# Hybrid decoder layer: attention outputs one unit later at step changes, row pieces in one run on GpSimd, and first output-stage tiles loaded from within attention

## The chip, the cores and the metric

The kernel runs on one core of one Trainium2 chip. The metric is the device time of one execution in microseconds. Engines are called PE (matmul), PEld (PE's weight loads), DVE (VectorE), ACT (ScalarE), POOL (GpSimd) and SP (the engine that issues nearly all DMAs).

## The reference, cut to what matters

One layer: an adaLN-modulated RMSNorm, one input projection, three mixers side by side (forgetting attention with 8 heads of 64, RWKV-7 with 4 heads, pooling), a SiLU gate, an output projection, a second RMSNorm and a gated residual. Sequence 4096, width 1024, batch 1. The change touches the attention and the seam to the output projection:

```python
s = jnp.einsum('bhqd,bhkd->bhqk', qh[:, :, q0:L], kh[:, :, :L])
s = s + cum[:, :, q0:L, None] - cum[:, :, None, :L]
p = jax.nn.softmax(jnp.where(causal, s, -jnp.inf), axis=-1)
outs.append(jnp.einsum('bhqk,bhkd->bhqd', p, vh[:, :, :L]))
...
y = jnp.concatenate([y_fox, y_rwkv, y_pool], axis=-1) * jax.nn.silu(g)
x = x + gate * rms_norm(y @ w_out[l], norm_post[l])
```

## The kernel before, in words

Five stages run one after the other, with a barrier of all engines between them: prepare, project, recur (RWKV and pooling), attend, output. They hand data on through scratch tensors in HBM: m.QK and m.V (queries, keys, values), m.G (gates), m.Y (mixer outputs before the gate).

**attend** (L1734 to L2268). A loop of TURNS = 4 turns does two heads each, u = 0 and 1. A head has NB = 8 blocks of 512 queries; block b of head u is a *step* s, 16 in a turn. A step goes over its 4(b+1) key tiles of 128; one key tile of a step is a *unit* k, NQK = 288 in a turn, 1152 in all. The list `start` holds the first unit of each step. On the last four units of a step, the causal diagonal, the width falls from 512 to 384, 256 and 128.

What one unit costs each engine:

- PE computes the scores psc (L2110 and L2112, and the mask product L2108 on the diagonal) into one of two PSUM banks; then the *ahead* work; then `output(k - PV_LAG)`: the product of probabilities and values of the unit five before (PV_LAG = 5), 8 matmuls at full width (L2091, L2093) into the two banks po, which hold all four query tiles of a step.
- ACT turns psc into p (the exponential, L2021, in one of NP = 8 buffers). At step changes it also copies po to oev (`evacuate`, two copies, L2013), after its exponential of unit start+4; PE may begin the po of the next step only then (the wait on o_ev in `output`, where x == 0).
- POOL computes plo, the low part of p that the second product needs (L1999), for three units of four; DVE does it for the fourth, k % 4 == 2 (L2224).
- DVE normalizes finished steps (`result`, `result_scaled`, L2230 to L2237).

The *ahead* work is how the softmax gets its maximum: PE computes a query-major score tile into one of NM = 4 banks pm (L2043, one for each unit, for a step AHEAD = 48 units on), DVE takes its maximum (L2164). When a step's maxima are all there its *row* is made: POOL adds an offset (`sums`, L1958, one unit after), DVE takes the largest (`largest`, L2244, two units after), POOL splits the result in three float16 pieces with seven small dependent operations (`pieces`, L1972 to L1984: four of them three units after, three of them four units after), PE transposes them into pm (`turn_row`, L2052, ROW_LAG = 7 units after) and DVE copies the row into qb (`copy_row`, L2191, COPY_LAG = 8). Each engine takes its instructions in the written order, so POOL's pieces stand ahead of the plo of their unit, and behind the wait for DVE's largest. Rows do not complete evenly: within a turn they are complete at units 11, 35, 63, 95, 99, 107, 119, 135 and at 144 more than each.

Before the loop stands a prologue with 48 such score tiles and the 4 rows that they complete. In it DVE does the row's steps itself: `m_step`, seven chained instructions (L2171 to L2183), then it waits for PE's transposes and copies.

At the start of attend SP loads qa, ka, the factors, qb, kb and v of head 0. At its end SP waits until the last attention outputs have landed in m.Y, then for its other loads, and the barrier follows.

**output** (L2271 to L2454). For each tile of 128 rows: load y, g and x, multiply y by g (DVE, L2418), scale, transpose (PE, L2390), split, and multiply by w_out (PE, L2397, 48 matmuls a tile), then norm and residual. Its tiles y, g, xr live in this stage alone, so SP loads the first three y and g and the first two x after the barrier (L2314 to L2319).

Of the kernel before, what the change touches and what calls it, by code (L numbers as in the profile page):

```python
# [19 lines left out]
F32 = mybir.dt.float32  # L20
# [700 lines left out]
def persistent(nc, ctx):  # L721
# [19 lines left out]
    m.cols = sb("cols", [P, 6 * KT])  # L741
    m.ab = sb("ab", [P, 3 * KT])
# [991 lines left out]
def attend(nc, a, m):  # L1734
# [5 lines left out]
    with ExitStack() as ctx:  # L1740
# [42 lines left out]
        AHEAD = 4 * NB + 16  # L1783
        PV_LAG = 5
        ROW_LAG, COPY_LAG, MSTEPS = 7, 8, 7
# [38 lines left out]
        pre, pre_row = 0, {}  # L1824
        for n, (s, t, q, c) in enumerate(early_items):
            pre += 1
            if t == CB - 1 and q == STEPS[s][1]:
                pre_row[s] = pre
                pre += 1
        use, row_use, NPM = {}, {}, 0  # L1830
# [36 lines left out]
        m_add, m_max, piece, o_sum = count("m_add", 16), count("m_max", 16), count("piece", 16 * 6), count("o_sum", 16)  # L1867
        dstep = count("a_dstep", NDV)

        with nc.Block() as block:  # L1870
            @block.sync
            def _(sp):
# [29 lines left out]
                load_second(0, 0)  # L1902
                with sp.Fori(0, TURNS) as i:
# [17 lines left out]
                for j in range(2):  # L1921
                    sp.wait_ge(out_d[j], 16 * 8 * TURNS)
# [5 lines left out]
            def _(pool):  # L1928
# [20 lines left out]
                pool.sem_inc(made, 1)  # L1949
                with pool.Fori(0, TURNS) as i:  # L1950
                    tt = nc.gpsimd.tensor_tensor

                    def sums(kc):

                        s = completes(kc)
                        u, b = STEPS[s]
                        pool.wait_ge(pm_d.sem, pm_d.past(i, pre + use[kc] + len(ahead(kc))))
                        tt(mt[:, :, 0:b + 1], mx[:, s, :, 0:b + 1],  # L1958
                           xr[:, u, b, 0:b + 1].unsqueeze(1).to_broadcast([P, CB, b + 1]), ALU.add).then_inc(m_add.sem, 1)

                    def pieces(kc, j0, j1):
# [3 lines left out]
                        a1, a2, a3 = (mw[:, side, :, XROW + n] for n in range(3))  # L1965
                        for j in range(j0, j1):
                            if j == 0:
                                pool.wait_ge(m_max.sem, m_max.past(i, done + 1))
                            else:
                                pool.wait_ge(piece.sem, piece.past(i, done * 6 + j))  # L1970
                            if j == 0:
                                tt(a1, mp[:, 0, :], fixed[:, 0, :], ALU.mult).then_inc(piece.sem, 1)  # L1972
# [570 lines left out]
```

## Time and profile before

| | us |
|---|---|
| median of 3 runs | 3676.57 (3675.87 to 3679.04) |
| the profiled execution | 3687.49 |
| its span | 3685.8 |

```profile
span 3685.8 us, 79815 instructions
PE 3469.7 (94%) x26404; PEld 2123.0 (58%) x26404; DVE 2266.1 (61%) x3715; ACT 1874.5 (51%) x3525; POOL 1601.9 (43%) x1996
PE   8999999999999996899999599999999999979998
DVE  7514142332424243787783599889988989974454
POOL 0112020211202022253553288888888888861222
PEclk9999999999999998798996699999999999989999
DMA  8111111111111112222220221020220211214555
L2091 PE MATMUL po<-v,p 128*128 128x129 f16 x4224 | 520.0, 220 | 35.7 <-ACT oev L2013 34.0
L2043 PE MATMUL pm<-ka,qa 128*128 128x512 f16 (+3 forms) x1200 | 439.1, 369 | 4.5 <-DVE mx L2164 4.4
```

The first line is the span, the second each engine's busy time. The digit strings cut the span in 40 slices of 92 us, each digit the busy share in tenths; PEclk is the granted clock of PE. Attention lies in slices 23 to 36, the output stage in the last four. The two last lines are groups of equal instructions: busy time and mean ns of one, then the idle time of the engine just before them and what ended it.

### The profile page before, as it was taken

The numbers are of one execution on the slowest core, as the hardware profiler recorded it, in microseconds if no ns is written. First come the engines' busy times: TensorE is split into PE (matmuls) and PEld (weight loads), VectorE is DVE, ScalarE is ACT, GpSimd is POOL, SyncE is SP. The second block draws the span as 40 slices with busy tenths as digits, with TensorE's granted clock in tenths as the row PEclk, the third lists the DMA queues.
The fourth block names the chain that finished last, engine by engine and source line by source line (L and its number), as shares of the span: only waits on it lengthen the run. The fifth ranks groups of instructions, "written<-read, shape, count | busy, mean of one in ns | idle before, by whom it ended". The sixth has DMA issues, their size and how long they took to land. (4 is left out here: it accounts for less than half of the span.)

```text
span 3685.8 us, 79815 instructions
## 1 busy us (share of the span) xinstructions
PE 3469.7 (94%) x26404; PEld 2123.0 (58%) x26404; DVE 2266.1 (61%) x3715; ACT 1874.5 (51%) x3525; POOL 1601.9 (43%) x1996
## 2 busy tenths in 40 slices
PE   8999999999999996899999599999999999979998
PEld 8444444444444443688888366666666656644454
DVE  7514142332424243787783599889988989974454
ACT  3323233222223233577774377777777767753333
POOL 0112020211202022253553288888888888861222
PEclk9999999999999998798996699999999999989999
DMA  8111111111111112222220221020220211214555
GB/s 327 52 52 69 64 52 64 55 62 55 66 58 60 64 55 75 61 83 66 66 58 25 55 55 40 23 57 9 54 57 8 57 23 41 57 68 160 182 186 183
DMA packets 211041, 267.81 MB, mean 73 GB/s; under 512 B 117309, under 2 KB 163092, under 8 KB 204212
## 3 DMA queue, kind: packets, MB, share of 16 engines
q1 hardware_dynamic: 210171, 262.65, 23.2%
q8 instruction: 223, 3.65, 0.4%
q14 instruction: 167, 1.37, 0.1%
q0 software_dynamic: 480, 0.14, 0.1%
HBM read 165.83 MB, written 96.89 MB: 71 GB/s over the span
## 5 line engine op out<-in xcount | busy, mean ns | idle before, releaser
L2021 ACT ACTIVATE p<-psc,xb,sc 128x512 f32<-128x512 f32 (+3 forms) x1152 | 855.1, 743 | 335.5 <-PE psc L2112 321.4
L1999 POOL TENSOR_TENSOR plo<-p 128x512 f16<-128x512 f32 (+2 forms) x864 | 888.0, 1051 | 150.8 <-ACT p L2021 147.0
L2164 DVE TENSOR_REDUCE mx<-pm 128x1 f32<-128x512 f32 (+3 forms) x1200 | 732.4, 637 | 96.4 <-PE pm L2043 84.8
L2091 PE MATMUL po<-v,p 128*128 128x129 f16 x4224 | 520.0, 220 | 35.7 <-ACT oev L2013 34.0
L2093 PE MATMUL po<-v,plo 128*128 128x65 f16 x4224 | 488.9, 192 | 0.0
L2091 PEld LDWEIGHTS po<-v,p 128*128 128x128 bf16 x4224 | 390.0, 97 | 140.6 <-POOL plo L1999 34.2
L712 POOL CAST stage<-qn 128x512 f16<-128x512 f32 x64 | 39.0, 609 | 968.6 <-DVE qn L597 968.6
L2043 PE MATMUL pm<-ka,qa 128*128 128x512 f16 (+3 forms) x1200 | 439.1, 369 | 4.5 <-DVE mx L2164 4.4
L2093 PEld LDWEIGHTS po<-v,plo 128*128 128x128 f16 x4224 | 379.6, 98 | 103.4
L2110 PE MATMUL psc<-qa,ka 128*128 128x512 f16 (+3 forms) x1152 | 419.1, 364 | 0.0
L2112 PE MATMUL psc<-qb,kb 128*128 128x512 f16 (+3 forms) x1152 | 417.9, 363 | 0.0
L438 PE MATMUL pmm<-hh,wh 128*128 128x512 f16 x1088 | 415.1, 382 | 0.3 <-DVE stage L615 0.2
L438 PE MATMUL pmm<-hl,wh 128*128 128x512 f16 x1088 | 414.9, 381 | 0.0
L438 PE MATMUL pmm<-hh,wl 128*128 128x512 f16 x1088 | 414.9, 381 | 0.0
L594 DVE RECIPROCAL rec<-stdb 128x512 f32<-128x512 f32 x64 | 214.5, 3351 | 188.0 <-ACT stdb L550 188.0
L2397 PE MATMUL pz<-wo,yh 128*128 128x512 f16 x1024 | 305.9, 380 | 3.1 <-DVE yl L2429 3.1
L438 PE MATMUL pmm<-wh,hh 128*128 128x512 f16 x768 | 291.1, 379 | 0.0
L438 PE MATMUL pmm<-wl,hh 128*128 128x512 f16 x768 | 291.1, 379 | 0.0
L438 PE MATMUL pmm<-wh,hl 128*128 128x512 f16 x768 | 291.1, 379 | 0.0
L2224 DVE TENSOR_TENSOR plo<-p 128x512 f16<-128x512 f32 (+1 forms) x288 | 268.7, 933 | 0.0
L620 DVE SCALAR_TENSOR_TENSOR stage<-pmm,sc,sig 128x512 f32<-128x512 f32 x64 | 48.0, 751 | 272.3 <-ACT sig L544 272.3
L2341 POOL TENSOR_TENSOR o<-o,xr 128x1024 f32<-128x1024 f32 x32 | 75.4, 2355 | 312.1 <-DVE o L2452 312.1
(357 smaller groups left out, 6003.0 us busy)
## 6 DMA issues: line engine op xcount, KB each, us to landing
xt<-in_x SPq DMA_DIRECT2D x36, 512.0 KB, 5.9
scratch_z<-stage SPq DMA_DIRECT2D x72, 256.0 KB, 2.0
y<-scratch_y SPq DMA_DIRECT2D x35, 512.0 KB
g<-scratch_g SPq DMA_DIRECT2D x35, 512.0 KB
xr<-in_x SPq DMA_DIRECT2D x34, 512.0 KB, 6.1
scratch_qk<-stage SPq DMA_DIRECT2D x64, 256.0 KB, 2.6
scratch_g<-stage SPq DMA_DIRECT2D x64, 256.0 KB, 2.0
out<-o SPq DMA_DIRECT2D x32, 512.0 KB, 3.0
```

What stands on the lines that cost most here:

```text
L438: mm = nc.tensor.matmul(out, lhs(l, k), rhs(r, k), start=(k == 0 and c == 0), stop=(k == KT - 1 and c == 2))
L594: nc.vector.reciprocal(rec[:], stdb[:]).then_inc(qk_rec.sem, 1)
L1999: nc.gpsimd.tensor_tensor(plo[:, k % NP, 0:w], p32[:, k % NP, 0:w], hi[:, 0:w], ALU.subtract)\
L2021: nc.scalar.activation(p32[:, k % NP, 0:w], psc[k % 2][:, 0:w], ACT.Exp, bias=xb[:, u, b, x // 4:x // 4 + 1], scale=m.sc[:, 0:1]).then_inc ...
L2043: ins = nc.tensor.matmul(pm[g][:, n, 0:w], qa[:, u, j * P:(j + 1) * P], ka[:, u, q * BT:q * BT + w], start=not last, stop=True, skip_group ...
L2091: nc.tensor.matmul(o[:, oc:oc + VW], hi[:, c0:c0 + P], v[:, u, x, 0:VW], start=(x == 0 and t % 2 == 0), stop=False, skip_group_check=True)
L2093: g = nc.tensor.matmul(o[:, oc:oc + 1 + HD], plo[:, k % NP, c0:c0 + P], v[:, u, x, 0:1 + HD], start=False, stop=(x == 4 * b + t), skip_gro ...
L2110: nc.tensor.matmul(psc[k % 2][:, 0:w], ka[:, u, ks], qa[:, u, t0:t0 + w], start=not diag, stop=False, skip_group_check=diag)
L2112: nc.tensor.matmul(psc[k % 2][:, 0:w], kb[:, u, ks], qb[:, u, t0:t0 + w], start=False, stop=True, skip_group_check=diag).then_inc(qk_mm.se ...
L2164: nc.vector.tensor_reduce(mx[:, s, t, q:q + 1], pm[g][:, 0, 0:w], AX.X, ALU.max).then_inc(pm_d.sem, 1)
L2224: tt(plo[:, k % NP, 0:w], p32[:, k % NP, 0:w], hi[:, 0:w], ALU.subtract).then_inc(lo_v.sem, 1)
L2397: mm = nc.tensor.matmul(pz[u % 2][j][:], l[:, u % 2, k // 4, ks], r[:, k, j * HALF:(j + 1) * HALF], start=(k == 0 and c == 0), stop=(k == ...
```

## The change

It does six things.

1. PE skips its output at unit start+5 of every step but the first of a turn, and does two at the next unit: that of unit start, then the usual one (both lines stand in the excerpt ahead of `output`).
2. POOL does all seven pieces of a row in one run, three units after the row completes.
3. AHEAD is 49 instead of 48, ROW_LAG 8 instead of 7, COPY_LAG 9 instead of 8. A row so completes one unit earlier (at units 10, 34, 62, 94, 98, 106, 118, 134), and its transposes and its copy stay at the same unit as before.
4. The prologue has 49 score tiles, and its four rows are made as in the loop: POOL does sum and pieces, DVE takes the largest two score tiles after the row's last, and PE's transposes and DVE's copy come seven score tiles after it (EARLY_LAG). DVE's m_step is gone.
5. The tiles y, g and xr of the output stage, and their semaphores, live from before attend. SP issues the loads of three g and two x tiles after attention's own first loads, and the loads of the three y tiles after the last store of attention, behind a wait for out_d[0] alone, ahead of the wait for out_d[1].
6. The output stage has no loads ahead of its loop.

```diff
--- before.py
+++ after.py
...
+    m.yg_in, m.xr_in = [sem(f"yg_in{s}") for s in range(4)], [sem(f"xr_in{s}") for s in range(4)]
...
-        AHEAD = 4 * NB + 16
+        AHEAD = 4 * NB + 17
         PV_LAG = 5
-        ROW_LAG, COPY_LAG, MSTEPS = 7, 8, 7
+        EARLY_LAG = 7
+        ROW_LAG, COPY_LAG = 8, 9
         EARLY_T = BT * (STEPS[units[AHEAD][0]][1] + 1)
...
-        pre, pre_row = 0, {}
+        pre, pre_row, pre_end, early, ends = 0, {}, {}, [], {}
         for n, (s, t, q, c) in enumerate(early_items):
+            early.append(("max", early_items[n]))
             pre += 1
             if t == CB - 1 and q == STEPS[s][1]:
-                pre_row[s] = pre
+                ends[n], pre_end[s] = s, pre
+            if n - 2 in ends:
+                early.append(("largest", ends[n - 2]))
+            if n - EARLY_LAG in ends:
+                early.append(("row", ends[n - EARLY_LAG]))
+                pre_row[ends[n - EARLY_LAG]] = pre
                 pre += 1
...
-        m_add, m_max, piece, o_sum = count("m_add", 16), count("m_max", 16), count("piece", 16 * 6), count("o_sum", 16)
+        m_add, m_max = count("m_add", 16, EARLY), count("m_max", 16, EARLY)
+        piece, o_sum = count("piece", 16 * 6, 6 * EARLY), count("o_sum", 16)
...
+                for t in range(3):
+                    sp.dma_start(m.g[:, t, :], m.G[t * P:(t + 1) * P, :]).then_inc(m.yg_in[t], 16)
+                    if t < 2:
+                        sp.dma_start(m.x[:, t, :], a.x[0, t * P:(t + 1) * P, :]).then_inc(m.xr_in[t], 16)
...
-                for j in range(2):
-                    sp.wait_ge(out_d[j], 16 * 8 * TURNS)
+                sp.wait_ge(out_d[0], 16 * 8 * TURNS)
+                for t in range(3):
+                    sp.dma_start(m.y[:, t, :], m.Y[t * P:(t + 1) * P, :]).then_inc(m.yg_in[t], 16)
+                sp.wait_ge(out_d[1], 16 * 8 * TURNS)
...
+                for r in range(EARLY):
+                    pool.wait_ge(pm_d.sem, pm_d.credit + pre_end[r])
+                    sum_of(r).then_inc(m_add.sem, 1)
+                    pool.wait_ge(m_max.sem, r + 1)
+                    for j in range(6):
+                        piece_of(j, r % 2).then_inc(piece.sem, 1)
+                        pool.wait_ge(piece.sem, r * 6 + j + 1)
+                    piece_of(6, r % 2).then_inc(row_d.sem, 1)
...
+                        sum_of(completes(kc)).then_inc(m_add.sem, 1)
+
+                    def pieces(kc):
...
+                        pool.wait_ge(m_max.sem, m_max.past(i, done + 1))
+                        for j in range(6):
+                            piece_of(j, side).then_inc(piece.sem, 1)
+                            pool.wait_ge(piece.sem, piece.past(i, done * 6 + j + 1))
+                        piece_of(6, side).then_inc(row_d.sem, 1)
...
                         if complete_at(k - 3):
-                            pieces(k - 3, 0, 4)
-                        if complete_at(k - 4):
-                            pieces(k - 4, 4, 7)
+                            pieces(k - 3)
...
-                for item in early_items:
+                n = 0
+                for what, item in early:
+                    if what == "largest":
+                        continue
                     pe.wait_ge(pm_d.sem, pm_d.credit + n + 1 - NM)
-                    by_query(n % NM, item)
+                    if what == "max":
+                        by_query(n % NM, item)
+                    else:
+                        turn_row(n % NM, item + 1, item % 2)
                     n += 1
-                    if item[1] == CB - 1 and item[2] == STEPS[item[0]][1]:
-                        rows += 1
-                        pe.wait_ge(pm_d.sem, pm_d.credit + n + 1 - NM)
-                        turn_row(n % NM, rows, (rows - 1) % 2)
-                        n += 1
...
                             turn_row(n % NM, i * NS + nth, (nth - 1) % 2)
+                        if k - PV_LAG in start[1:NS]:
+                            continue
+                        if k - (PV_LAG + 1) in start[1:NS]:
+                            output(k - (PV_LAG + 1))
                         if k >= PV_LAG:
                             output(k - PV_LAG)
...
@@ -2163,25 +2194,6 @@
                     w = min(BT, (4 * b + t + 1) * P - q * BT)
                     nc.vector.tensor_reduce(mx[:, s, t, q:q + 1], pm[g][:, 0, 0:w], AX.X, ALU.max).then_inc(pm_d.sem, 1)
 
-                def m_step(j, s, side):
...
+                for what, item in early:
+                    if what == "largest":
+                        dve.wait_ge(m_add.sem, item + 1)
+                        largest_of(item).then_inc(m_max.sem, 1)
+                        continue
+                    if what == "max":
+                        maximum(n + 1, item, n % NM)
+                    else:
+                        copy_row(n + 1, item, n % NM)
                     n += 1
-                    if item[1] == CB - 1 and item[2] == STEPS[s][1]:
-                        rows += 1
-                        dve.wait_ge(pm_d.sem, pm_d.credit + n)
-                        for j in range(MSTEPS - 1):
-                            chain(m_step(j, s, (rows - 1) % 2))
-                        m_step(MSTEPS - 1, s, (rows - 1) % 2).then_inc(row_d.sem, 1)
-                        copy_row(n + 1, s, n % NM)
-                        n += 1
...
-                        b, done = STEPS[completes(kc)][1], rows_before(kc + 1) - 1 - EARLY
-                        dve.wait_ge(m_add.sem, m_add.past(i, done + 1))
-                        nc.vector.tensor_reduce(mp[:, 0, :], mt[:, :, 0:b + 1], AX.X, ALU.max).then_inc(m_max.sem, 1)
+                        dve.wait_ge(m_add.sem, m_add.past(i, rows_before(kc + 1) - EARLY))
+                        largest_of(completes(kc)).then_inc(m_max.sem, 1)
...
-        y, g, x = (sb(n, [P, UN, DM]) for n in ("y", "g", "xr"))
+        y, g, x = m.y, m.g, m.x
...
-                for t in range(UN - 1):
-                    r = slice(t * P, (t + 1) * P)
-                    sp.dma_start(y[:, t, :], m.Y[r, :]).then_inc(yg_in[t], 16)
-                    sp.dma_start(g[:, t, :], m.G[r, :]).then_inc(yg_in[t], 16)
-                    if t < 2:
-                        load_x(t, t)
...
+        m.y = ctx.enter_context(nc.sbuf_tensor("y", [P, 4, DM], F32))
+        m.g = ctx.enter_context(nc.sbuf_tensor("g", [P, 4, DM], F32))
+        m.x = ctx.enter_context(nc.sbuf_tensor("xr", [P, 4, DM], F32))
         attend(nc, a, m)
...
```

`piece_of(j, side)` and `sum_of(s)` hold POOL's same eight operations as before, now called from both places; `largest_of` is DVE's reduction L2244.

## Rows read from the trace of the kernel before

**Rows 1.** Busy time by stage: prologue with start, head loop, one turn; columns first

```profile
core 0: us, PE busy (x) PEld busy (x) DVE busy (x) ACT busy (x) POOL busy (x), PEclk, DMA share, GB/s
2040.00:2105.00 65.00, 25.77 (x100) 11.07 (x100) 36.30 (x83) 15.04 (x31) 14.90 (x24) 0.58 0.31 75
2105.00:3295.00 1190.00, 1122.25 (x12673) 734.86 (x12672) 1071.75 (x1784) 883.51 (x1280) 1026.75 (x1376) 0.99 0.17 38
2402.00:2700.00 298.00, 280.60 (x3168) 183.85 (x3168) 267.94 (x446) 220.98 (x320) 256.69 (x344) 0.99 0.17 38
```

**Rows 2.** Waits in the head loop: waiter <- releaser: us, times, longest

```profile
POOL plo L1999 <- ACT p L2021: 147.0, 156, 42.4
...
PE po L2091 <- ACT oev L2013: 34.0, 60, 0.7
...
PE pm L2052 <- POOL mw L1984: 16.8, 24, 1.1
```

**Rows 3.** Timeline, PE, step change in turn 2: start, us, work [idle <-releaser]

```profile
2489.53 0.38 PE L2110 MATMUL psc<-qa,ka 128*128 128x512 f16 x1
...
2490.89 0.23 PE L2091 MATMUL po<-v,p 128*128 128x129 f16 x1 [0.55 <-ACT oev L2013]
...
2491.24 0.38 PE L2110 MATMUL psc<-qa,ka 128*128 128x512 f16 x1
...
2492.24 0.38 PE L2110 MATMUL psc<-qa,ka 128*128 128x512 f16 x1
```

**Rows 4.** Timeline, ACT, at the same step change: copies, next exponential but one

```profile
2490.11 0.65 ACT L2013 ACTIVATE oev<-po 128x258 f32<-128x258 f32 x2
...
2491.88 0.78 ACT L2021 ACTIVATE p<-psc,xb,sc 128x512 f32<-128x512 f32 x1 [0.45 <-PE psc L2112]
```

**Rows 5.** Timeline, PE, where rows complete 4, 8 and 12 units apart

```profile
2502.26 0.39 PE L2043 MATMUL pm<-ka,qa 128*128 128x512 f16 x1 [0.51 <-DVE mx L2164]
...
2504.99 0.40 PE L2052 MATMUL pm<-id,mw 128*128 128x128 f16 x4 [0.45 <-POOL mw L1984]
...
2510.41 0.40 PE L2052 MATMUL pm<-id,mw 128*128 128x128 f16 x4 [1.09 <-POOL mw L1984]
...
2518.81 0.40 PE L2052 MATMUL pm<-id,mw 128*128 128x128 f16 x4 [0.56 <-POOL mw L1984]
```

**Rows 6.** Timeline, POOL, in the same stretch

```profile
2493.73 3.66 POOL L1999 TENSOR_TENSOR plo<-p 128x512 f16<-128x512 f32 x3 [0.78 <-ACT p L2021]
...
2502.72 0.21 POOL L1972 TENSOR_TENSOR mw<-mp,fixed 128x4 f16<-128x4 f32 x1 [1.10 <-DVE mp L2244]
...
2504.87 1.04 POOL L1999 TENSOR_TENSOR plo<-p 128x512 f16<-128x512 f32 x1
...
2525.06 1.04 POOL L1999 TENSOR_TENSOR plo<-p 128x512 f16<-128x512 f32 x1 [0.35 <-ACT p L2021]
```

**Rows 7.** Timeline, DVE: a plo beside one of POOL's, and one without

```profile
2489.48 1.57 DVE L2224 TENSOR_TENSOR plo<-p 128x512 f16<-128x512 f32 x1
...
2498.81 0.67 DVE L2224 TENSOR_TENSOR plo<-p 128x512 f16<-128x512 f32 x1
```

**Rows 8.** Timeline, DVE, prologue around the third early row

```profile
2081.11 6.47 DVE L2164 TENSOR_REDUCE mx<-pm 128x1 f32<-128x512 f32 x12
...
2089.89 0.43 DVE L2191 COPY qb<-pm 32x512 f16<-32x512 f16 x1 [0.88 <-PE pm L2052]
2090.35 8.86 DVE L2164 TENSOR_REDUCE mx<-pm 128x1 f32<-128x512 f32 x16
```

**Rows 9.** Timeline, all engines, from attention to the output stage

```profile
3296.39 0.37 SPq L1915 DMA_DIRECT2D scratch_y<-osb  x1
3299.31 0.38 SPq L2316 DMA_DIRECT2D y<-scratch_y  x1
...
3304.26 1.23 DVE L2418 TENSOR_TENSOR y<-y,g 128x1024 f32<-128x1024 f32 x1 [8.11 <-DMA g<-scratch_g]
...
3314.60 1.03 PE L2397 MATMUL pz<-wo,yh 128*128 128x512 f16 x2 [3.13 <-DVE yl L2429]
```

More of the change, by code:

```diff
@@ L1949, in _, with sum_of, piece_of @@
                 pool.sem_inc(made, 1)
+                tt = nc.gpsimd.tensor_tensor
+                def sum_of(s):
+                    u, b = STEPS[s]
+                    return tt(mt[:, :, 0:b + 1], mx[:, s, :, 0:b + 1],
+                              xr[:, u, b, 0:b + 1].unsqueeze(1).to_broadcast([P, CB, b + 1]), ALU.add)
+                def piece_of(j, side):
+                    a1, a2, a3 = (mw[:, side, :, XROW + n] for n in range(3))
+                    if j == 0:
+                        return tt(a1, mp[:, 0, :], fixed[:, 0, :], ALU.mult)
+                    if j == 1:
+                        return tt(mb[:, 0, :], a1, fixed[:, 1, :], ALU.mult)
+                    if j == 2:
+                        return tt(mp[:, 1, :], mb[:, 0, :], mp[:, 0, :], ALU.add)
+                    if j == 3:
+                        return tt(a2, mp[:, 1, :], fixed[:, 2, :], ALU.mult)
+                    if j == 4:
+                        return tt(mb[:, 1, :], a2, fixed[:, 3, :], ALU.mult)
+                    if j == 5:
+                        return tt(mp[:, 2, :], mb[:, 1, :], mp[:, 1, :], ALU.add)
+                    return tt(a3, mp[:, 2, :], fixed[:, 4, :], ALU.mult)
@@ L1953, in sums @@
                     def sums(kc):
-                        s = completes(kc)
-                        u, b = STEPS[s]
                         pool.wait_ge(pm_d.sem, pm_d.past(i, pre + use[kc] + len(ahead(kc))))
-                        tt(mt[:, :, 0:b + 1], mx[:, s, :, 0:b + 1],
-                           xr[:, u, b, 0:b + 1].unsqueeze(1).to_broadcast([P, CB, b + 1]), ALU.add).then_inc(m_add.sem, 1)
-                    def pieces(kc, j0, j1):
+                        sum_of(completes(kc)).then_inc(m_add.sem, 1)
@@ L2195, in _, with largest_of @@
                 head_vectors(chain, 0, 0, chain)
[L2196 to L2208 removed]
+                def largest_of(s):
+                    b = STEPS[s][1]
+                    return nc.vector.tensor_reduce(mp[:, 0, :], mt[:, :, 0:b + 1], AX.X, ALU.max)
+                n = 0
+                for what, item in early:
[7 more added lines that the diff above has]
+                        copy_row(n + 1, item, n % NM)
+                    n += 1
                 with dve.Fori(0, TURNS) as i:
@@ L2287, in output @@
         pz = [[ps(f"pz{s}{j}") for j in range(2)] for s in range(2)]
-        yg_in = [sem(f"yg_in{s}") for s in range(UN)]
-        xr_in = [sem(f"xr_in{s}") for s in range(UN)]
+        yg_in, xr_in = m.yg_in, m.xr_in
         gated, sq_d, norm_d, inv_d, scaled = (count("o_" + n, 1) for n in ("gated", "sq_d", "norm_d", "inv_d", "scaled"))
```

43 lines of the change are left out of this document (1 added, 42 removed).

## The prediction

> **What bounds the kernel now.** I read the busy time by stage first [rows 1]. In the head loop PE is busy 1122.3 of 1190 us at a granted clock of 0.99, so the loop runs at PE's pace and its idle time, 68 us, is what can be won there. The turn row says who stands close behind: of 298 us DVE is busy 268 and POOL 257. Then the list of waits [rows 2]: PE idled 34.0 us in 60 waits for ACT's copies of po, one for each step change but the first of a turn (15 by 4), and 16.8 us in 24 waits for POOL's row pieces. POOL in turn waited 147 us for exponentials, so it had room, though not everywhere.
>
> The timeline shows what such a wait costs. Scores of one unit to scores of the next normally take 2491.24 to 2492.24, 1.00 us; at the step change they take 2489.53 to 2491.24, 1.71 us [rows 3]. The idle time shown is 0.55, the cost 0.71 us, some 0.2 more, because an idle PE also loses the overlap of weight loads. ACT's two copies end at 2490.76 and PE starts at 2490.89 [rows 3, 4].
>
> Where rows complete close together another limit shows: PE waits 0.51 for a maximum and 0.45, 1.09, 0.56 for pieces [rows 5], and POOL, after a wait of 1.10 for DVE's largest at 2502.72, has no wait until 2525.06 [rows 6]. That stretch (two a turn, eight in all) goes at POOL's pace.
>
> **Late outputs.** PE skips one output at unit start+5 and does two at start+6. Without the stall that unit holds only scores and the ahead tile, some 0.65 us (1.00 less an output's 0.35, which is 2490.89 to 2491.24 of [rows 3]). ACT's copies end 1.23 us after the scores of start+5 begin (2489.53 to 2490.76). PE now asks for them 0.65 + 0.65 = 1.30 us after. They just fit. The exponential of start+5, queued behind the copies on ACT, takes 0.78 [rows 4] and ends at about 2.0 us; PE needs its bank at start+7, at 0.65 + 0.65 + 2 x 0.35 = 2.00. So the next wait in line is on that bank and is worth 0 to 0.1 us. What gives way behind PE: the value product of start comes a unit later, and nothing waits for it but its p buffer, of which there are eight. I put 0.71 us for each of the 52 step changes outside the dense stretches: 36.9 us gained. The lower bound is zero (the wait moves), the upper 0.75 each.
>
> **The dense stretches.** Before, a stretch cost PE 0.51 + 0.45 + 1.09 + 0.56 and 0.2 more for each of the four waits, 3.4 us [rows 5], and with the step change at unit 117 that lies in it 4.1 us. The edit asks for the same POOL work. Seven pieces in one run took 2502.72 to 2504.87, 2.15 us [rows 6]. They were already one run there but for the unit that DVE makes low, so the run itself costs nothing; being asked one unit earlier, with the transposes at the same unit, gives the pieces about 2 us of slack more. The row waits as such go. What is late next is the plo queued behind the pieces on POOL, for which PE waits. Its slack: an exponential ends 1.42 us after its scores begin (2491.24 to 2492.66), a plo takes 1.04, PE asks for it 5.65 us after, so POOL may be 3.2 us behind. Three plo in four units take 3.1 (3 x 1.04) to 3.66 us [rows 6], so in 4 us POOL catches up 0.3 to 0.9. Three rows in 12 units add 6.45 and give back 0.9 to 2.7: 3.8 to 5.6 against 3.2, a stall of 0.6 to 2.4 us. The fourth, 12 units later, adds -0.5 to 1.25, and not below nothing: 0.6 to 3.6 together, 2.1 in the middle. DVE's wait with its 0.2 stays (0.7). So 2.8 after against 4.1 before: 1.3 us gained in each, 10.4 us in eight; bounds -1.6 and 22.
>
> **DVE.** With 12 us less in a turn DVE is busy 268 of 286 us, 94%. It must not be more than the four pm banks behind PE. Where it lost PE 0.51 us before [rows 5], I let it lose as much again in each half turn: 4 us lost; bounds 0 and 8. The head loop so gives 36.9 + 10.4 - 4 = 43 us.
>
> **Prologue.** DVE stood between the maxima of one step and of the next from 2087.58 to 2090.35 [rows 8], 2.77 us, in four rows 11.1 us. Afterwards it does there a copy of 0.43 and the largest, some 0.2, so 0.65 with the joints. Whether it also waits: POOL's pieces need 2.15 us and the transposes 0.88 [rows 6, 8], 3.0 us, while five maxima of 8.86 / 16 = 0.55 cover 2.8. I take 0.5 us of waiting for a row (bounds 0 and 1.5), and the 49th tile costs 0.55. Gain: 11.1 - 4 x 1.15 - 0.55 = 6 us; bounds 1.9 and 7.9. POOL has nothing else to do there: 14.9 of 65 us busy [rows 1].
>
> **The first tiles.** SP's five loads of g and x stand behind all first loads of attention in SP's queue, and in front of a wait that is only met when the first step is done. DMA is busy 0.31 in that window [rows 1]. I cost them at nothing; if the cover were gone they would hold back nothing that PE asks for before the v of head 0, a few us once at most. At the end the y loads go out right behind the last store, from 3296.8 instead of 3299.31; three issues of 0.38 end at 3298.0, ahead of the 3299.31 at which SP passes the barrier [rows 9]. DVE began at 3304.26, 4.95 us after the first y was issued with g behind it. Now y lands alone between 3299.3 (it is there at the barrier) and 3301.8 (it takes the 4.95 too). Gain 2.5 to 5.0, I take 4. What comes after, 10.3 us to the first product at 3314.60, stays as it is: it is DVE, ACT and PE in turn, none of which waits for a load. A rule of the Trainium skill bears on this: "DMA: Bandwidth & Descriptors", Anatomy of one DMA (told there for GpSimd's path), gives a transfer a fixed cost of about 2 us, most of it the receipt of the last write. By it the y tile would be in at the barrier and the gain here 5 and not 4 us; no row before shows a y load alone.
>
> **The sum.** 43 + 6 + 4 = 53 us. The profiled execution took 3687.5 us, 1.7 more than its span and 11 more than the median; from it the sum gives 3634, and from the median of 3676.6, which is what will be measured against, 3623 us.
>
> **Rivals.**
>
> - A. POOL and DVE take up half of what is freed. For it: the busy shares of a turn [rows 1]. Against: POOL waits for ACT at 2493.73, three units after a step change [rows 6]. Then 18 us at the step changes, nothing in the dense stretches, 4 lost to DVE, 4 and 3 at the ends: 21 us, 3655.
> - B. Slower, by collisions of DVE and POOL. DVE's plo takes 1.57 us beside one of POOL's and 0.67 without [rows 7], and POOL's three take 3.66 and not 3.12 [rows 6]. If denser queues make one more in each four units collide, POOL gets 72 x 0.5 = 36 us more work a turn: 293 us, and with some 8 idle at the turn's head 301 to 306 against 298 now. In four turns that is 12 to 32 us more, with 10 saved at the ends 3689 in the middle. It decides from about 42 more collisions a turn (286 - 257 - 8 = 21 us of room, 0.5 each). The Trainium skill has the rule: "SBUF — State Buffer", SBUF: two separate sides, says that a DVE operation with two SBUF inputs and a GpSimd operation that reads SBUF exclude each other for a whole instruction. The trace agrees with its 1.57 beside 0.67. Against it: such operations are as many as before.
> - C. Everything goes: 60 x 0.71, the 3.4 of all eight stretches, 8 and 5 at the ends: 83 us, 3594. For it: the row waits are waits for pieces, not for plo. Against it: POOL's work without a gap of 22 us [rows 6].
> - D. The late output doesn't do what it says, and the wait only moves to the exponential's bank, since need and end both lie at 2.0 us. Then 10 us at the ends and 2 in the stretches are left: 3665.
>
> **Chances.** Forecast 0.56, A 0.21, C 0.12, D 0.06, B 0.05. The range must hold 0.8: from 3602, which takes in the forecast with its larger gains (22 us in the dense stretches in place of 10, 8 and 5 at the ends) and the edge of C, to 3656, which takes in A. Left out are most of C, D and B. All cases but B are faster by over 0.2% (7 us, about what a measurement of this kernel can tell from no change), and of D a third may fall within it: faster 0.93, same 0.02, slower 0.05.
>
> **What would show it.** PE po waiting for ACT oev gone from the list of waits (under 5 us), else D. PE pm waiting for POOL mw gone, and in its place PEld po waiting for plo at units 101 and 109 of each half turn, some 2 us together: more than 4 is A. In the prologue 0.4 to 1 us in front of each copy on DVE, and POOL's pieces there. The first y multiply at about 3300 on the old scale. POOL's plo at 1.05 us in the mean: 1.2 would be B. The prediction fails if DVE, not PE, ends most waits of the loop: then PE pm waits for DVE mx would exceed 15 us.

## The result and the profile after

| | before | after |
|---|---|---|
| median of 8 runs each, us | 3676.2 (3666.3 to 3684.7) | 3658.4 (3638.3 to 3668.7) |
| ratio | | 0.9942, 95% interval 0.9921 to 0.9962 |
| the profiled execution | 3687.5 | 3661.0 |
| its span | 3685.8 | 3659.3 |

The change gains 0.6% (14 to 29 us of 3676; the medians are 18 apart). The forecast was 53 us. By stage, from the first and last starts of the instructions that bound each stage:

| stage | before | after | forecast |
|---|---|---|---|
| up to the first pm product, code not changed | 2069.0 | 2072.0 | 0 |
| prologue, to the first score product | 36.0 | 29.1 | -6 |
| head loop, first to last score product | 1186.4 | 1166.1 | -43 |
| seam, to the first product with w_out | 23.2 | 19.7 | -4 |
| output stage | 371.2 | 372.3 | 0 |

In the three parts that it touches the change saves 30.7 us: 6.9 in the prologue, 20.3 in the loop and 3.5 at the seam.

The stages ahead of attention scatter: in the profiles of both kernels and of the eleven kernels below they end between 2041 and 2072 us, all with the same code up to there. The granted clock goes along with it. Over the first 2040 us it is 0.95 in the profiles before and after, and 0.96 in that of e7, which reaches attention 28 to 31 us sooner. In 53 further executions of the kernel before, the time runs from 3659.6 us at a mean granted clock of 0.969 to 3697.7 at 0.956, some 3 us for each 0.001. At like clock, 0.960 to 0.962, sixteen of them have a median of 3684.4 us and four of the changed kernel one of 3656.5. They are from other sessions, so this is an estimate: it puts the gain at 28 us, near the 30.7 of the stages, and suggests that the two sets of eight fell on somewhat different clocks.

So I compare the parts of attention by their own length, and totals by the intervals alone. Each kernel has one profile. The one pair with the same loop code, the change and e7 below, has prologues of 29.1 us both and loops 1.8 us apart, so a difference of 2 us in the loop says little.

The head loop's length stands in one line of each trace: the rows of the score product by source line, with its duration ns min/median/max, then the first and last start. Before, then after:

```profile
L2110 PE MATMUL psc<-qa,ka x1152: 219/380/634, 2105.0 to 3291.4; 128*128 128x512 f16 x192
```

```profile
L2137 PE MATMUL psc<-qa,ka x1152: 219/380/634, 2101.1 to 3267.3; 128*128 128x512 f16 x192
```

The changed kernel's list of waits in the head loop (us in total, times, longest) answers [rows 2]:

```profile
DVE mx L2195 <- PE pm L2070: 80.7, 164, 5.4
POOL plo L2026 <- ACT p L2048: 64.3, 89, 6.4
PEld po L2118 <- POOL plo L2026: 29.5, 56, 0.8
POOL mt L1971 <- DVE mx L2195: 25.4, 32, 1.6
...
PE po L2118 <- POOL plo L2026: 19.5, 48, 0.7
...
PE pm L2079 <- POOL mw L1989: 6.0, 16, 0.7
```

The 34.0 us for ACT's copies are gone, and PE's wait for pieces fell from 16.8 to 6.0 us. In their place PE waits 19.5 us for POOL's plo, where it waited 1.7 before. POOL's own room shows in its wait for exponentials: 147 us before, 64.3 now. Of the 147, however, 42.4 are a single wait that ends at 2107.1, ahead of POOL's first plo of the loop, so within the loop it was 105. One turn by the busy-time view, with its columns (PE, PEld, DVE, ACT, POOL, clock), answers the last line of [rows 1]:

```profile
2394.10:2687.70 293.60, 281.85 (x3168) 183.14 (x3168) 265.07 (x446) 219.14 (x320) 258.11 (x344) 0.99 0.17 39
```

And the page's groups show plo dearer on both engines, from 1051 to 1077 ns on POOL and from 933 to 996 ns on DVE. Before, then after:

```profile
L1999 POOL TENSOR_TENSOR plo<-p 128x512 f16<-128x512 f32 (+2 forms) x864 | 888.0, 1051 | 150.8 <-ACT p L2021 147.0
...
L2224 DVE TENSOR_TENSOR plo<-p 128x512 f16<-128x512 f32 (+1 forms) x288 | 268.7, 933 | 0.0
```

```profile
L2026 POOL TENSOR_TENSOR plo<-p 128x512 f16<-128x512 f32 (+2 forms) x864 | 906.0, 1077 | 66.2 <-ACT p L2048 64.3
...
L2239 DVE TENSOR_TENSOR plo<-p 128x512 f16<-128x512 f32 (+1 forms) x288 | 286.8, 996 | 0.0
```

**A step change, after.** PE's timeline at unit 89 of turn 2, and ACT's:

```profile
2480.24 0.38 PE L2137 MATMUL psc<-qa,ka 128*128 128x512 f16 x1
...
2480.97 0.39 PE L2137 MATMUL psc<-qa,ka 128*128 128x512 f16 x1
...
2482.32 0.38 PE L2137 MATMUL psc<-qa,ka 128*128 128x512 f16 x1
```

```profile
2478.41 2.51 ACT L2048 ACTIVATE p<-psc,xb,sc 128x512 f32<-128x512 f32 x3 [0.22 <-PE psc L2139]
2480.81 0.65 ACT L2040 ACTIVATE oev<-po 128x258 f32<-128x258 f32 x2
```

From the scores of unit 89 to those of unit 91 it is now 2.08 us; in [rows 3] it was 2.71. The late output does what it says.

**Where PE waits now.** To see each unit I took the time from one score product's weight load to the next, less the columns that PE pushes in between at 2.4 GHz (the granted clock of the loop is 0.99), less 0.033 us (the median unit has that much). What is left is lost time. Of turn 2, in us, by units:

| units | before | after | late alone (e1) | rows alone (e2) | spread (e4) | three pieces (e5) |
|---|---|---|---|---|---|---|
| 5 to 24 | 1.7 | 2.3 | 1.9 | 1.8 | 0.5 | 1.0 |
| 24 to 95 | 2.9 | 0.6 | 0.9 | 3.0 | 1.5 | 0.3 |
| 95 to 120, dense | 4.0 | 3.5 | 3.4 | 4.1 | 1.2 | 0.6 |
| 120 to 144 | 0.2 | 0.5 | 0.6 | 0.1 | 0.4 | 0.1 |
| 144 to 164 | 2.2 | 1.6 | 1.6 | 2.3 | 0.4 | 0.6 |
| 164 to 239 | 2.9 | 0.6 | 0.9 | 3.0 | 0.4 | 0.5 |
| 239 to 264, dense | 3.9 | 3.2 | 3.2 | 3.8 | 1.6 | 0.6 |
| 264 to 287 | 0.3 | 0.5 | 0.7 | 0.1 | 1.8 | 0.1 |
| turn's end and head | 6.4 | 6.7 | 7.8 | 7.2 | 6.9 | 5.8 |
| sum | 24.4 | 19.5 | 20.9 | 25.3 | 14.8 | 9.3 |

A clean step change fell from 0.72 to 0.08. But units 18 and 162 lose 1.2 us each that they didn't lose before. There the timelines of PE, POOL and DVE read together:

```profile
2412.10 0.40 PE L2079 MATMUL pm<-id,mw 128*128 128x128 f16 x4 [0.67 <-POOL mw L1989]
```

```profile
2406.86 0.41 POOL L1971 TENSOR_TENSOR mt<-mx,xraw 128x20 f32<-128x20 f32 x1 [1.59 <-DVE mx L2195]
2407.23 1.39 POOL L2026 TENSOR_TENSOR plo<-p 128x128 f16<-128x128 f32 x2
2409.66 0.21 POOL L1978 TENSOR_TENSOR mw<-mp,fixed 128x4 f16<-128x4 f32 x1 [1.04 <-DVE mp L2211]
...
2411.99 3.39 POOL L2026 TENSOR_TENSOR plo<-p 128x512 f16<-128x512 f32 x3
```

```profile
2403.03 1.55 DVE L2239 TENSOR_TENSOR plo<-p 128x512 f16<-128x512 f32 x1
```

POOL stood still twice, 1.59 us for the last maximum and 1.04 us for DVE's largest, with plo queued behind it, and then had 2.3 us of pieces to do. DVE was likely late for that maximum in part because of POOL: its plo ahead of it took 1.55 us beside POOL's, where 0.67 is the time of one alone (see the last section). In the dense stretch PE waits for plo as well as for pieces:

```profile
2495.09 0.23 PE L2118 MATMUL po<-v,p 128*128 128x129 f16 x1 [0.51 <-POOL plo L2026]
2499.49 0.40 PE L2079 MATMUL pm<-id,mw 128*128 128x128 f16 x4 [0.19 <-POOL mw L1989]
2500.46 0.23 PE L2118 MATMUL po<-v,p 128*128 128x129 f16 x1 [0.58 <-POOL plo L2026]
2509.21 0.23 PE L2118 MATMUL po<-v,p 128*128 128x129 f16 x1 [0.66 <-POOL plo L2026]
```

**Prologue and seam.** DVE around the third early row, which answers [rows 8]:

```profile
2087.84 0.15 DVE L2211 TENSOR_REDUCE mp<-mt 128x4 f32<-128x12 f32 x1
2087.92 2.67 DVE L2195 TENSOR_REDUCE mx<-pm 128x1 f32<-128x512 f32 x5
2090.85 0.43 DVE L2203 COPY qb<-pm 32x512 f16<-32x512 f16 x1 [0.26 <-PE pm L2079]
```

The seam, which answers [rows 9]; the last store is issued 23.98 us earlier than there:

```profile
3272.41 0.37 SPq L1929 DMA_DIRECT2D scratch_y<-osb  x1
3273.00 1.32 SPq L1937 DMA_DIRECT2D y<-scratch_y  x3
...
3276.64 1.22 DVE L2425 TENSOR_TENSOR y<-y,g 128x1024 f32<-128x1024 f32 x1 [4.46 <-DMA y<-scratch_y]
...
3286.98 1.03 PE L2404 MATMUL pz<-wo,yh 128*128 128x512 f16 x2 [3.13 <-DVE yl L2436]
```

### The profile page after: what moved, and what is told of

The parts are those of the page before. It is cut to its first block and busy times, and to the rows that moved or that the text cites. A ratio compares the mean times of both kernels' runs of the same rounds, so it can differ in the third digit from the quotient of the medians.

```text
span 3659.3 us, 79839 instructions
## 1 busy us (share of the span) xinstructions
PE 3477.6 (95%) x26405; PEld 2124.3 (58%) x26405; DVE 2252.1 (62%) x3692; ACT 1866.7 (51%) x3525; POOL 1613.3 (44%) x2028
## 3 DMA queue, kind: packets, MB, share of 16 engines
q14 instruction: 170, 1.39, 0.1%
## 5 line engine op out<-in xcount | busy, mean ns | idle before, releaser
L2026 POOL TENSOR_TENSOR plo<-p 128x512 f16<-128x512 f32 (+2 forms) x864 | 906.0, 1077 | 66.2 <-ACT p L2048 64.3
L2118 PE MATMUL po<-v,p 128*128 128x129 f16 x4224 | 513.5, 220 | 22.8 <-POOL plo L2026 19.5
L2118 PEld LDWEIGHTS po<-v,p 128*128 128x128 bf16 x4224 | 388.8, 97 | 124.9 <-POOL plo L2026 29.5
L2239 DVE TENSOR_TENSOR plo<-p 128x512 f16<-128x512 f32 (+1 forms) x288 | 286.8, 996 | 0.0
```

The costliest lines, as they stand in the source:

```text
L2026: nc.gpsimd.tensor_tensor(plo[:, k % NP, 0:w], p32[:, k % NP, 0:w], hi[:, 0:w], ALU.subtract)\
L2118: nc.tensor.matmul(o[:, oc:oc + VW], hi[:, c0:c0 + P], v[:, u, x, 0:VW], start=(x == 0 and t % 2 == 0), stop=False, skip_group_check=True)
L2239: tt(plo[:, k % NP, 0:w], p32[:, k % NP, 0:w], hi[:, 0:w], ALU.subtract).then_inc(lo_v.sem, 1)
```

## Experiments: which part, and which engine

Three theories. Q: POOL and DVE are at their limit in stretches, and PE's saved time comes back there as waits. M: the late outputs only move the wait. R: what was done to the rows (one run, one unit earlier) does the harm. From e9 on theory P says that POOL's room limits the change. Each kernel's head loop is read from the same line as above, and each total is its ratio to executions of the kernel before in the same session, with the 95% interval.

**e1, late outputs alone** on the kernel before.

```diff
+                        if k - PV_LAG in start[1:NS]:
+                            continue
+                        if k - (PV_LAG + 1) in start[1:NS]:
+                            output(k - (PV_LAG + 1))
                         if k >= PV_LAG:
                             output(k - PV_LAG)
```

> The kernel before with the late outputs alone (rows, lags, prologue and loads as before). Looked at: the head loop, from the start of the first score product (psc) to that of the last, 1186.4 us before and 1166.2 with the whole change. Theory Q (queues): a step change itself costs PE 0.66 us less (1.71 to 1.05), but in the stretches where rows complete close together POOL and DVE are the limit, and the time comes back there as waits for row pieces and plo. Then the loop is some 13 us shorter, 1170 to 1177, and PE's waits for pieces grow over the 16.8 us of before. Rival M (moved wait): the late output frees little in itself since PE then waits for the bank that the exponential holds: loop over 1181. Rival R (the rows' part does the harm: one run on POOL, one unit earlier): without it the full gain of some 40 us shows: loop under 1155.

Loop 1166.7 us, total 0.9954 of before (0.9926 to 0.9981). Its waits in and just ahead of the loop:

```profile
PE pm L2052 <- POOL mw L1984: 28.2, 48, 1.1
```

Pieces now cost 28.2 us in place of 16.8 [rows 2]. M and R are out: the loop is neither over 1181 nor under 1155. It is shorter than Q's 1170 to 1177, a miss too, and as long as with the whole change. So the late outputs brought all of the loop's 20 us, and the rest of the change nothing.

**e2, rows, prologue and loads without the late outputs**: the changed kernel less the four lines above.

> The changed kernel without the late outputs: rows in one run on POOL, AHEAD 49, lags 8 and 9, prologue and loads as changed. Theory Q: the row waits of before (some 3.4 us in a half turn with DVE's) get somewhat shorter, nothing gets longer, since the step changes still give POOL and DVE their pauses: head loop 1172 to 1182, total 12 to 25 us less than before (6.9 of it in the prologue, 3.6 at the seam to the output stage). Rival R: the new wait for pieces at units 18 and 162 (1.2 us each) is there without the late outputs too, and the loop is not shorter than 1184. Rival M expects the loop within 3 us of that of the whole change, 1163 to 1169.

Loop 1189.0 us, 2.6 more than before; total 0.9964 (0.9941 to 0.9988). Q (1172 to 1182) and M (1163 to 1169) miss the loop. R's number holds, not under 1184, but its reason doesn't: unit 18 has no wait. Its waits:

```profile
PE po L2118 <- ACT oev L2040: 33.8, 60, 0.6
PE po L2118 <- POOL plo L2026: 14.8, 32, 0.7
PE pm L2079 <- POOL mw L1989: 3.0, 9, 1.5
```

The earlier pieces turned 16.8 us of waits for pieces into 3.0, and gave back 14.8 as waits for plo. The dense stretches cost 4.1 and 3.8 us as before (table), so the rows part gained nothing there either. In addition the mean plo rose as in the whole change, 1074 ns on POOL and 1004 on DVE, while e1 has 1059 and 910. The dearer plo comes with the rows part, not with the late outputs.

**e3, pieces in two runs again**: four at three units after the row and three at four, in the changed kernel.

```diff
-                            pieces(k - 3)
+                            pieces(k - 3, 0, 4)
+                        if complete_at(k - 4):
+                            pieces(k - 4, 4, 7)
```

> The changed kernel with the pieces split over two units again (four at three units after the row completes, three at four). Theory Q: POOL's work is the same, so the loop stays within 3 us of the whole change, 1163 to 1169, with waits shifted between plo and pieces. Rival R: a run of seven ahead of a plo is what PE waits for, and the loop falls under 1158.

Loop 1164.9 us, 1.2 less than the whole change and so the same, total 0.9905 (0.9879 to 0.9931). PE's waits for pieces are 28.2 us and those for plo 1.1. One run or two decides only whether PE waits for pieces or for plo. R, which had the loop under 1158, falls.

**e4, the same work with the rows taken up evenly.** complete_at and completes look a row up in a table; nothing else is changed. Most rows are taken up later than they are complete, and further apart.

```diff
+        ROW_AT = {22: 4, 40: 5, 62: 6, 94: 7, 108: 8, 120: 9, 133: 10, 150: 11,
+                  168: 12, 186: 13, 206: 14, 238: 15, 248: 0, 258: 1, 268: 2, 278: 3}
```

> The changed kernel, with the rows taken up later and evenly: at units 22, 40, 62, 94, 108, 120, 133, 150, 168, 186, 206, 238, 248, 258, 268, 278 of a turn and not at the units where they complete (10, 34, 62, 94, 98, 106, 118, 134 and 144 more). All work is the same, every row is still there before its step. Theory Q: what is lost is lost to backlog, so most of the waits at units 18, 102, 106, 114, 126 and their twins go, and the head loop falls from 1166 to 1145 to 1153 us, the total by 13 to 21 us against the whole change. Rivals M and R: the loop stays within 4 us of 1166. If POOL or DVE lacks time on the whole turn and not only in stretches, the waits spread out too, and the loop stays over 1158.

Loop 1147.5 us, total 0.9863 (0.9814 to 0.9913). This is Q's number. The waits at 18, 106 and 114 are gone; those at 99 and 102 stay, and new ones of up to 1.0 us stand at 35, 50, 266 and 286. So 18.6 us of the loop had hung on where the rows stand, for two reasons (table): the dense stretches give 3.9 us of a turn, and units 5 to 24 and 144 to 164 give 3.0, where the row doesn't stand close to another but right between two step changes, at 9 and 17.

**e5, less work on POOL.** Three of the seven piece operations stay; the second and third piece are zero. In the exact arithmetic of the softmax the number taken off in numerator and denominator alike has no effect, so what is left out is the fine part of the maximum.

```diff
-                for n_, value in enumerate((-1.0 / TOP, TOP, -1.0 / 32, 32.0, -32.0)):
+                for n_, value in enumerate((-1.0 / TOP, TOP, 0.0, 32.0, 0.0)):
...
-                        for j in range(6):
+                        for n_, j in enumerate((0, 3)):
```

> The changed kernel with less work on POOL: three of a row's seven piece operations (the second and third piece are zero, so the maximum taken off is the rounded one). About 1.1 us less for each of 16 rows in a turn. Looked at: PE's time over its columns, unit by unit, and the head loop (1166.1 us with the whole change). Theory Q says that two engines limit in different places: POOL where rows complete 4 to 12 units apart, DVE at units 18 and 162, where POOL idled 1.59 and 1.04 us for DVE. So the waits at units 102, 106, 114, 126 fall from 3.6 us in a half turn to under 1.5, those at 18 and 162 stay near 1.1, and the loop is 1143 to 1156 us. If DVE is the limit everywhere, the loop stays over 1160.

Loop 1127.2 us, 38.9 less than the whole change and far below Q's 1143 to 1156; total 0.9802 (0.9760 to 0.9844). The edit took some 70 us of piece operations off POOL (four of 0.28 us for each of 64 rows). The waits at 102 to 126 are gone, and so, against the expectation, is most of the one at unit 18 (1.2 to at most 0.3), with DVE's work untouched: POOL still stands idle 0.96 and 1.04 us for DVE there, but has only three pieces to do after it. PE's waits in the loop:

```profile
PE po L2118 <- DVE plo L2239: 3.5, 14, 0.3
PE pm L2070 <- DVE mx L2195: 1.6, 6, 0.3
```

**e6, less work on DVE.** The two operations that finish a step handle one query tile of four, so three quarters of the attention output are zero. (POOL clears osb once at the start.)

```diff
-                        tt(osb[:, s % 2, :, :], o4[:, :, 1:1 + HD], o4[:, :, 1 + HD:VW], ALU.add)
+                        tt(osb[:, s % 2, 0:1, :], o4[:, 0:1, 1:1 + HD], o4[:, 0:1, 1 + HD:VW], ALU.add)
```

> The changed kernel with less work on DVE: the two operations that finish a step handle one of its four query tiles (the rest of the attention output is zero). They took 0.86 and 0.76 us in the mean, and have two inputs in SBUF each, as POOL's plo has. Theory Q: the waits at units 18 and 162 (1.2 us each) go to under 0.5, the ones at 102, 106 and 114 shrink by less than half, since they are POOL's, and the loop is 1150 to 1158 us. If DVE is the limit everywhere the dense stretches empty too, and the loop is under 1145. If POOL is, 18 and 162 stay and the loop is over 1162.

Loop 1158.5 us, 7.6 less than the whole change, total 0.9892 (0.9853 to 0.9930). None of the three expectations for the loop holds; Q's 1150 to 1158 is missed by half a microsecond. Unit 18 falls to 0.8 only (in turn 2 it stays at 1.3), and the dense stretches stay (3.2 and 3.4). The edit took less off DVE than it seems to: the two groups, 768 and 603 ns in the mean with the whole change, are still

```profile
L2248 DVE TENSOR_TENSOR osb<-oev 128x64 f32<-128x64 f32 x64 | 36.2, 566 | 0.0
L2253 DVE SCALAR_TENSOR_TENSOR osb<-osb,sc,rl 128x64 f32<-128x64 f32 x64 | 29.3, 458 | 0.1
```

That is 22 us off DVE, and its plo got 12 us dearer (996 to 1039 ns in the mean), against the 70 us that e5 took off POOL. So e5 shows that POOL's pieces are a limit, at unit 18 too. e6 shows that DVE has a share, and is too small a cut to say how large; how the two compare stays open.

**e7, loads after the barrier** as before, all else as changed.

```diff
-                sp.wait_ge(out_d[0], 16 * 8 * TURNS)
-                for t in range(3):
-                    sp.dma_start(m.y[:, t, :], m.Y[t * P:(t + 1) * P, :]).then_inc(m.yg_in[t], 16)
-                sp.wait_ge(out_d[1], 16 * 8 * TURNS)
+                for j in range(2):
+                    sp.wait_ge(out_d[j], 16 * 8 * TURNS)
```

> The changed kernel with the output stage's first tiles loaded after the barrier, as before. All theories: the head loop and the prologue as with the whole change (1166 and 29.1 us, within 1), so the early g and x loads cost the start of attention nothing; the seam from the last score product to the first product with w_out back from 19.7 to 23.2 us.

Prologue 29.1 us, loop 1164.3, seam 23.2; total 0.9921 (0.9889 to 0.9952). The early loads are worth their 3.5 us and cost the start of attention nothing. The loop differs by 1.8 us, more than I allowed. Its code is that of the whole change, so this is what the loop scatters by.

**e8, the rows moved once more.**

```diff
+        ROW_AT = {24: 4, 47: 5, 66: 6, 99: 7, 113: 8, 124: 9, 136: 10, 151: 11,
+                  168: 12, 186: 13, 206: 14, 238: 15, 247: 0, 256: 1, 265: 2, 278: 3}
```

> The evenly spread rows (loop 1147.5 us) with some moved again, to units 24, 47, 66, 99, 113, 124, 136, 151, 168, 186, 206, 238, 247, 256, 265, 278: away from the step change at 45 and from the start of the next head's vectors on DVE at 95, and with the last ones further apart. Theory Q: of the 1.5 us a turn left between units 24 and 60, 0.96 at 95 to 112 and 2.0 at 264 to 287, about half goes: loop 1138 to 1145 us. If what is left isn't from rows but from the two engines' total work, it stays at 1146 to 1149.

Loop 1152.2 us, 4.7 more than e4; total 0.9876 (0.9836 to 0.9917). A miss. The waits at units 35 and 50 went, new ones of 0.9 us came at 74 and 273, and the one at 99 grew from 0.5 to 1.3. What is left after spreading can't be placed by this kind of reading.

**e9, three pieces without the late outputs**: e5 less the four lines of e1.

> The changed kernel with three of the seven piece operations on POOL (loop 1127.2 us with them) and without the late outputs. It asks what a late output is worth when POOL has room. Theory P (POOL's room is what limits the change): 60 step changes at 0.66 us come back in full, the loop is 1160 to 1168 us, against 1186.4 before and 1189.0 for the changed kernel without late outputs. Then late outputs are worth 33 to 41 us here, where they were worth 20 to 23 with all seven pieces. If the step changes are worth less than the timeline says, the loop is under 1153.

Loop 1161.3 us, as expected, total 0.9881 (0.9846 to 0.9917), with the old wait back:

```profile
PE po L2118 <- ACT oev L2040: 33.8, 60, 0.6
```

So late outputs are worth 34.1 us with three operations (1161.3 to 1127.2), 22.9 with all seven (e2 to the whole change, 1189.0 to 1166.1), and 19.7 on the kernel before (e1). Where POOL has room they come nearest to their price one by one: 34.1 us are 0.57 for each of the 60, against 0.63 in the timeline and the 0.71 of the forecast.

**e10, a single piece operation.** The edit is against e5.

```diff
-                        for n_, j in enumerate((0, 3)):
-                            piece_of(j, side).then_inc(piece.sem, 1)
-                            pool.wait_ge(piece.sem, piece.past(i, done * 2 + n_ + 1))
-                        piece_of(6, side).then_inc(row_d.sem, 1)
+                        piece_of(0, side).then_inc(row_d.sem, 1)
```

> The changed kernel with a single piece operation for a row on POOL: the maximum taken off is rounded to float16, the second and third piece stay zero. The same number is taken off in numerator and denominator of the softmax, so the result does not hang on the two others. Theory P: another 0.56 us less for each row, little of it left to win, since after three operations only 1.5 us of waits a turn are left between units 5 and 264: loop 1122 to 1127 us, total 0.975 to 0.982 of before.

Loop 1135.6 us, total 0.9823 (0.9793 to 0.9852). Less work on POOL, and yet 8.4 us more than e5: theory P's 1122 to 1127 is missed. PE's wait for DVE's plo grew from 3.5 us to 6.8:

```profile
PE po L2112 <- DVE plo L2233: 6.8, 19, 0.5
```

plo is at 1092 ns on POOL and 1027 on DVE in the mean, dearer than in e5 (1085, 1017). Perhaps POOL's and DVE's operations meet more often; that was not tested.

**e11, three pieces and rows spread.**

> The changed kernel with three piece operations on POOL and the rows taken up evenly. Spreading gave 18.6 us of the loop with seven piece operations (1166.1 to 1147.5), three operations 38.9 (to 1127.2). Theory P: both act on the same thing, POOL's backlog, and with three operations only about 1.5 us a turn are left between units 5 and 264, so spreading gives 0 to 6 us more: loop 1121 to 1128 us. Were they independent, it would be about 1109.

Loop 1129.8 us, total 0.9837 (0.9798 to 0.9877). The two don't add up: 2.6 us more than e5 alone, where independent gains would have given 1109. That fits theory P, by which both act on POOL's backlog; by 2 us it lies outside the range.

e5 has the shortest loop. Its total beats the kernel before and the changed one by its interval (0.9760 to 0.9844), at the price of the fine part of the maximum; from e10 and e11 the totals don't tell it apart.

## Why the prediction was wrong

The sign was right, and the size was off: 18 us of median (14 to 29 by the ratio), and 30.7 in the stages of the one trace, against 53. Rival A came within 3 us of the median, at 3655 against 3658.4, and in part by luck: it had 14 us for the loop and 7 for the ends, where the stages show 20.3 and 10.4. Its mechanism, POOL and DVE taking up half of what is freed, is what the runs bear out, and the prediction's own sign for it showed: it allowed PEld some 2 us of waits for plo and called more than 4 rival A. PEld has 29.5 us, and PE itself 19.5 where it had 1.7.

- **Prologue, -6.** Measured 36.0 to 29.1, -6.9. Right. The copies wait 0.26 to 0.33 us where I took 0.5.
- **Early loads, -4 at the seam, nothing at the start.** Measured -3.5, and e7 shows both. The y multiply begins 4.2 us after the store's issue (3272.41 to 3276.64) where it was 7.9. The first y tile was in at most 3.6 us after its own issue (3273.00 to 3276.64), between the two cases that the forecast stood on. The prediction's sentence by the Trainium skill ("DMA: Bandwidth & Descriptors", Anatomy of one DMA) took only the fixed 2 us of that section, which adds a term for the data; with it, an estimate for 512 KB is 3.2 us, the tile would not have been in at the barrier, and the trace is nearer to that.
- **A late output, 0.71 us.** Nearly right locally: 2.71 to 2.08 us, 0.63, with PE's request for the copies 1.39 us after the scores (forecast 1.30). A short wait for an exponential has come (0.4 us of PEld at the scores of unit start+6), since on the narrow diagonal units PE goes faster than ACT's 0.84 us a piece.
- **52 step changes outside the dense stretches, 36.9 us.** This is the step that failed. From the table, units 5 to 95 and 144 to 239 gave 4.7 us in turn 2; the same reading of all four turns gives 20.0. More than half of the 16.9 that are missing is the new wait at units 18 and 162: 8 times 1.2, 9.3 us. Some 4 more are the 52 changes at 0.63 in place of 0.71, and the rest are waits of under 0.2 us near units 10, 42 and 70 and their twins. I had held the slack of 3.2 us against three rows in a row and taken for granted that one row alone fits. I had counted only the 2.15 us of the run. POOL also stood still 1.59 and 1.04 us for DVE ahead of it, in order, with plo behind; these pauses belong to a row's price. Before the change the stalls of the step changes at 9 and 17 had covered them: the wait is there with the late outputs alone (e1) and not without them (e2). e5 shows that POOL's pieces are needed for it, and e4 that it goes when the row stands elsewhere.
- **Dense stretches, 4.1 to 2.8.** Measured 4.0 and 3.9 to 3.5 and 3.2. The account by slack and backlog named the right engine and the right new wait, for plo, though at units 101 and 109 and not at 102, 106, 114 and 126, and took the middle of 0.6 to 3.6 where the truth lay near the upper end. What was gained is the step change at 117, not the row waits (e2 has 4.1 and 3.8). The 0.3 us more at 120 to 144 and again at 264 to 287 belongs to it: the backlog lasts longer than the stretch.
- **DVE, 4 us lost.** The new waits at 126 and 270 were of about that size, but are POOL's. PE's waits that end with DVE stayed small, 2.6 us for its plo and 2.2 for a maximum, and taking 22 us of its work away (e6) gave 7.6 us. The "147 us" by which POOL seemed to have room held the 42.4 ahead of the loop.
- **Collisions (rival B).** The plo on both engines did get dearer, as B's mechanism has it, by 26 ns on POOL and 63 on DVE. Over 864 and 288 of them that is 22 and 18 us of work. It didn't come from denser queues but with the rows part (e2 has it, e1 doesn't), and so that part, which I had credited with 10 us in the loop (5.7 of them the step changes at 117), gave none. That a shift by one unit changes how the two engines' operations meet is the likely cause; it was not tested alone.

In short: I added up what each wait cost PE, and the sum held only as far as the next engine had room. 257 of 298 us busy looked like 41 us of room in a turn. With three piece operations the late outputs gave 34.1 us and with all seven 22.9: the room was missing where it counted.

## What to carry to other kernels

When a pause of the bounding engine is removed, the engines that used it to catch up lose it too: work out, unit by unit, where each of them is behind, with the pauses in which it waits in order counted as its work. A share of busy time of 86% over a turn can be a limit if its work comes in bunches or right after a pause that is gone; moving the rows (18.6 us) was worth about as much as all that the change did for PE in the loop, and cutting POOL's work (38.9 us) twice as much. And test a term alone before adding the next: late outputs were worth 20, 23 or 34 us by what stood beside them.

## What the hardware showed that I had not expected

- POOL's and DVE's plo, both with two inputs in SBUF, don't run side by side. Where spans overlap, the one that starts first keeps its own length, and the other lasts until a fixed time after the first has ended. Before, in turn 2, POOL first, then DVE first (the second POOL row holds two operations; the first of them takes 1.34 us):

```profile
2465.67 1.04 POOL L1999 TENSOR_TENSOR plo<-p 128x512 f16<-128x512 f32 x1 [0.78 <-ACT p L2021]
2482.05 2.34 POOL L1999 TENSOR_TENSOR plo<-p 128x512 f16<-128x512 f32 x2 [0.30 <-ACT p L2021]
```

```profile
2465.80 1.45 DVE L2224 TENSOR_TENSOR plo<-p 128x512 f16<-128x512 f32 x1
2481.82 0.68 DVE L2224 TENSOR_TENSOR plo<-p 128x512 f16<-128x512 f32 x1
```

  In the 56 pairs of the kernel before in which a full-width plo of DVE meets just one of POOL's, DVE's ends 0.55 us after POOL's in nearly all of the 44 with POOL first, however far apart they began, and POOL's 0.90 us after DVE's in all 12 with DVE first. So the pair costs nearly the sum of both, 0.67 and 1.04 us, and the second one's long span is mostly waiting. That is the rule of the Trainium skill that the prediction names under rival B ("SBUF — State Buffer", SBUF: two separate sides), and the trace agrees. The mean thus depends on the order of quite other work: 910 to 1040 ns on DVE and 1051 to 1092 on POOL over the kernels.
- A chain of dependent 128x4 operations on POOL costs 0.28 us each (0.20 of work and 0.08 to the next; now and then one takes 0.6 to 0.7), so seven cost as much as two plo of 128x512.
- Less work on POOL can make the loop longer (e10, 1135.6 against 1127.2 us).
- The stages ahead of attention took between 2041 and 2072 us over the profiles, with the same code, and by and large the longer they took the lower was the granted clock. Up to 1380 us it is 0.99 or more in all of them; the lower values come behind that, from 1380 to 1840 us 0.89 before and 0.92 in e7. What lowers the clock in one execution more than in another is open.
